# Two transformer blocks in fp32 on one core: heads retimed, SSD decay by a selector, both ends reworked, operand tiles moved to 512-byte starts

## The reference, cut to what matters

```
first block
  h = x + [SSD(32 heads, conv, gate z) | short conv] @ w_out      # hybrid mixer
      decay = exp(where(causal, a_cs[l] - a_cs[s], -inf))         # a_cs: cumulative sum of dt*a over tokens
      scores = (C @ B.T) * decay ;  y = scores @ (x * dt) + x * d_skip
  h = h + cross_attention(4 heads, 256 memory tokens)
  h = h + swiglu(h);  h = rmsnorm(h)
second block
  q,k,v of three kinds of heads:
      8 differential heads (two softmaxes each), 8 stick-breaking heads, 8 band heads with a relative bias
  each head's output normalised; x = x + y @ w_o
  x = x + swiglu with a causal conv on the gate;  out = rmsnorm(x) * final_norm_2
```

## Time and profile before

| | |
|---|---|
| median of three runs | 2810.08 us |
| profiled execution | 2806.39 us |
| its span, first to last instruction | 2804.6 us |
| mean granted TensorE clock | 0.997 |
| TensorE busy | 2757.1 us (98%) |
| VectorE busy | 1952.7 us (70%) |
| ScalarE busy | 1284.8 us (46%) |
| HBM read | 494.41 MB, 177 GB/s over the span |

### The profile page before, as it was taken

One profiled execution on the slowest core, in us unless ns is written; L12 is line 12 of the kernel. 1 busy time (PEld: TensorE's weight loads), 2 busy tenths in 40 slices (PEclk: granted clock), 3 DMA queues, 4 the chain that ended last, 5 costly groups with the idle time before them and its releaser, 6 DMA issues.

```text
span 2804.6 us, 40399 instructions
## 1 busy us (share of the span) xinstructions
PE 2757.1 (98%) x16796; PEld 2434.7 (87%) x16796; DVE 1952.7 (70%) x2416; ACT 1284.8 (46%) x1632; POOL 90.9 (3%) x67
## 2 busy tenths in 40 slices
PE   8999999999999999999999999999999999999997
PEld 7888999888888888888888888788898888888886
DVE  7777777766767665666566886576687757775775
ACT  5444545554555443444344544454454433443443
POOL 1000000000201000000000110000010000000002
PEclk9999999999999999999999999999999999999999
DMA  6555554346555555555555554344455555565553
GB/s 234 187 185 185 172 179 143 121 144 220 184 165 171 190 195 192 184 193 192 191 188 191 191 175 159 128 158 135 151 175 193 195 191 185 181 204 191 186 192 120
DMA packets 137622, 499.16 MB, mean 178 GB/s; under 512 B 15312, under 2 KB 16344, under 8 KB 137312
## 3 DMA queue, kind: packets, MB, share of 16 engines
q1 hardware_dynamic: 135792, 492.20, 52.5%
q10 hardware_dynamic: 1648, 4.39, 0.4%
HBM read 494.41 MB, written 2.11 MB: 177 GB/s over the span
## 4 chain that ended last, share of the span: by engine, by line
PE 94%; DVE 3%; ACT 2%; issue 0%; DMA 0%; DVEq 0%; ACTq 0%
PE PS L477 94%; DVE wlo L1201 1%; ACT whi L819 1%; DVE AR L1507 0%; DVE X L1635 0%; ACT AR L997 0%; DVE X L1677 0%; DMA X<-in_x 0%; PE PS L554 0%; DVE X L1633 0%; ACT AR L1065 0%; DVE H L1195 0%; DVE AR L1349 0%; DVE AR L1343 0%; DVE AR L1516 0%
## 5 line engine op out<-in xcount | busy, mean ns | idle before, releaser
L477 PE MATMUL PS<-H,whi 128*128 128x512 f32 (+1 forms) x5472 | 1787.0, 380 | 12.9 <-DVE wlo L1201 11.5
L1201 DVE TENSOR_TENSOR wlo<-raw,whi 128x1024 fp32r<-128x1024 f32 x930 | 1130.6, 1231 | 681.8 <-ACT whi L819 678.6
L819 ACT ACTIVATE whi<-raw 128x1024 fp32r<-128x1024 f32 x930 | 972.1, 1057 | 984.4 <-PE PS L477 956.3
L477 PE MATMUL PS<-H,wlo 128*128 128x256 f32 x5072 | 1413.8, 279 | 0.0
L477 PEld LDWEIGHTS PS<-H,whi 128*128 128x128 f32 x5472 | 1002.5, 188 | 220.8 <-issue 17.0
L477 PEld LDWEIGHTS PS<-H,wlo 128*128 128x128 f32 x5072 | 957.5, 189 | 2.0 <-issue 1.7
L477 PE MATMUL PS<-Y,whi 128*128 128x512 f32 (+1 forms) x2240 | 717.9, 376 | 1.1 <-DVE X L1635 0.8
L477 PE MATMUL PS<-Y,wlo 128*128 128x256 f32 x2048 | 569.0, 278 | 0.0
L477 PEld LDWEIGHTS PS<-Y,whi 128*128 128x128 f32 x2240 | 407.7, 188 | 83.9 <-DVE X L1635 2.0
L477 PEld LDWEIGHTS PS<-Y,wlo 128*128 128x128 f32 x2048 | 385.5, 188 | 0.2
L1507 DVE TENSOR_REDUCE AR<-PS 128x512 f32<-128x1024 f32 x140 | 171.5, 1225 | 14.6
(11 more groups left out here) (160 smaller groups left out, 961.9 us busy)
## 6 DMA issues: line engine op xcount, KB each, us to landing
raw<-in_ffn SPq DMA_DIRECT2D x528, 512.0 KB, 4.4
raw<-in_w_in SPq DMA_DIRECT2D x178, 512.0 KB, 4.5
raw<-in_w_qkv SPq DMA_DIRECT2D x96, 512.0 KB, 3.8
raw<-in_w_out SPq DMA_DIRECT2D x64, 512.0 KB, 4.4
raw<-in_w_o SPq DMA_DIRECT2D x40, 512.0 KB, 3.8
raw<-in_w_q SPq DMA_DIRECT2D x8, 512.0 KB, 3.9
raw<-in_w_k SPq DMA_DIRECT2D x8, 512.0 KB, 3.8
raw<-in_w_v SPq DMA_DIRECT2D x8, 512.0 KB, 4.7
```

The source lines that it names most:

```text
L477: return e.matmul(out, l, r, start=start, stop=stop)
L819: a.then_inc(e.activation(c.whi[:, s % NW, :], c.raw[:, s % NRAW, :], ACT.Copy), "whi")
L1201: v.then_inc(e.tensor_tensor(c.wlo[:, s % NW, :], c.raw[:, s % NRAW, :], c.whi[:, s % NW, :].bitcast(F32), ALU.subtract), "wlo")
```

## The change

It has five parts.

1. **Timetable.** The slots of `xa`, `dfa`, `dfb`, `stk` and `bnd` are new, with some `idle` counts one larger; waits for V, K and Q name the tile that a head needs, where before they named all tiles.
2. **SSD decay.** The `dt` task now makes the cumulative sums as rows: 32 rows of high parts, 32 of low parts, and the rest zero, in `ACS`. `SEL` is a matrix of 128 rows whose column h picks the rows of head h. A head takes one matmul of 384 columns and one of 2 x 128 for the mask. On VectorE the two instructions that add `d_skip` on the diagonals become one.
3. **Start.** The 16 gains come with `x` in one DMA, the first half of weights comes and is split in two parts, ScalarE's table is loaded before it waits, and the first four blocks wait for the first part alone.
4. **End.** ScalarE multiplies `x` by the final gain as tiles are finished; norm 6 starts three slots ahead of the end with its first two matmuls; the last table load is moved ahead; VectorE does six instructions of 512 columns and GpSimd two, and eight output DMAs of 256 KB are issued by SyncE and ScalarE.
5. **Addresses.** A tile `gap` of 384 bytes is put ahead of `raw`, and `x` with the gains (`XG`) goes behind all others. `raw`, `whi`, `wlo`, `H`, `Y` and `CR` begin at multiples of 512 bytes; they moved by 384 bytes, `H`, `Y` and `CR` by 384 bytes less 16384.

```diff
-    out += [(first_slot("wv") + 2 + 2 * h, "xa", h) for h in range(4)]
+    out += [(first_slot("wv") + s, "xa", h) for h, s in enumerate((-5, -3, 3, 5))]
...
-    out += [(v + s, "dfa", h) for h, s in enumerate((0, 5, 10, 15, 39, 44, 49, 54))]
-    out += [(after("va") + s, "dfb", h) for h, s in enumerate((1, 5, 9, 13, 24, 28, 32, 36))]
...
+    out += [(v + 7 * h, "dfa", h) for h in range(8)]
+    out += [(v + 7 * h + 13, "dfb", h) for h in range(8)]
+    out += [(v + s, "stk", i) for i, s in enumerate((57, 71, 85, 99))]
+    out += [(v + s, "bnd", i) for i, s in enumerate((105, 114, 124, 136))]
+    out += [(first_slot("g1") + 4, "norm", 5), (N_SLOT - 3, "norm", 6)]
...
+        sb("gap", [P, 96])
         self.raw = sb("raw", [P, NRAW, SUB])
...
-        self.X = sb("X", [P, 16 * T])
...
-        self.ADT = sb("ADT", [P, 4, 32], F32R)
+        self.SEL = sb("SEL", [P, 32], F32R)
         self.AR = AR = sb("AR", [P, 17352])
+        self.XG = sb("XG", [P, 16 + 16 * T])
...
     def ssd(i):
...
-            mm(bank[:, 0:384], w0[0], c.TRIr, True, False)
-            mm(bank[:, 0:384], w0[1], c.TRIr, False, False)
-            for q in range(2):
-                for o in (128, 256):
-                    mm(bank[:, o:o + 128], w1[q], c.TRIr[:, 0:128], False, False)
-            mm(bank[:, 0:128], c.Ir, c.MNr, False, False)
-            p.then_inc(mm(bank[:, 256:384], c.Ir, c.MNr, False, True), "ssd_dec")
+            mm(bank[:, 0:384], c.SEL[:, h:h + 1].to_broadcast([P, P]), c.ACS, True, False)
+            ends = bank.rearrange("p (a b) -> p a b", a=2)[:, :, 0:128]
+            p.then_inc(mm(ends, c.Ir, c.MNr.unsqueeze(1).to_broadcast([P, 2, P]), False, True), "ssd_dec")
...
     def dt(_):                                    # TensorE
+        row = bank[0:64, 128:384]
+        for o in (0, 32):
+            mm(row[o:o + 32, :], c.adt[:, 0:32], c.tri[:, 0:256], True, False)
+        for o in (0, 32):
+            last = mm(row[o:o + 32, 128:256], c.adt[:, 32:64], c.tri[:, 0:128], False, True)
...
     def bnd(i):                                   # TensorE, output of the band heads
-        for j in range(2):
-            p.wait_ge(*done("vc", j))
+        p.wait_ge(*done("vc", i // 2))
...
+        if stage == "d12":                        # ScalarE, leave
+            a.wait_ge(*a.at)
+            for k in (2 * j, 2 * j + 1):
+                a.then_inc(e.activation(c.xt(k), c.xt(k), ACT.Copy, scale=c.col("final_norm_2", k)), "scaled")
+            if j == 6:
+                load(LN_EXP)
...
-    for k in range(16):                           # VectorE, the end
-        if k % 4:
-            v.then_inc(e.scalar_tensor_tensor(c.xt(k), c.xt(k), c.col("final_norm_2", k), c.RN, ALU.mult, ALU.mult), "gain_x")
+    for i in range(6):
+        v.wait_ge("scaled", 2 * i + 2)
+        v.then_inc(times(c.xt(2 * i, 2), c.xt(2 * i, 2), c.RN), "gain_x")
```

More of the change, by code:

```diff
@@ L463, in sync_program @@
         load(w)
[L464 to L468, removed]
+    for i in range(6):
+        s.wait_ge("gain_x", i + 1)
+        e.dma_start(c.out[:, 2 * i * T:(2 * i + 2) * T], c.xt(2 * i, 2)).then_inc(c.sems["out"], 16)
+    s.wait_ge("out", 128)
     s.wait_ge("rows", 16)
@@ L484, in take, with norm_mm @@
         return c.misc[b]
[L486 to L491, removed]
+    def norm_mm(bank, s, start, stop, cols):
+        mm(bank[:, 0:T], c.ones, s[:, 0:T], start, False)
+        last = mm(bank[:, 0:T], c.ones, s[:, T:2 * T], False, stop)
         if cols:
@@ L503, in norm @@
         p.wait_ge("sum_add", 7 * n + (6 if n == 6 else 7))
+        last = norm_mm(bank, c.SUM, True, n != 6, n in (3, 4))
         if n == 6:
+            yield from idle(3)
             p.wait_ge("sq", 8 * n + 8)
-        p.then_inc(norm_mm(bank, c.SUM, c.SQ[1] if n == 6 else None, n in (3, 4)), "norm_sum")
+            last = norm_mm(bank, c.SQ[1], False, True, False)
+        p.then_inc(last, "norm_sum")
         yield
@@ L599, in xa @@
         p.then_inc(last, "xa_s")
-        yield from idle(5)
+        yield from idle(6)
         bank = take("xa", h, "t")
@@ L607, in xa @@
         p.then_inc(last, "xa_turn")
-        yield from idle(XA_PV[h] - 5)
+        yield from idle(XA_PV[h] - 6)
         bank = take("xa", h, "o")
@@ L719, in bnd @@
             p.then_inc(last, "bnd_turn")
-        yield from idle(3)
+        yield from idle(4)
         bank = take("bnd", i, "o")
-        for j in range(2):
-            p.wait_ge(*done("vc", j))
+        p.wait_ge(*done("vc", i // 2))
         for n, WT in enumerate((P0, P1)):
@@ L841, in norm @@
         _, r, col = norm_dst(c, n)
-        yield
+        yield from idle(3 if n == 6 else 1)
         if col is not None:
@@ L902, in dt @@
         a.then_inc(e.activation(ab, u1, ACT.Ln), "dt_a")
+        yield from idle(17)
+        row = c.bank("dt", 0, "n")[0:64, 128:384]
+        a.wait_ge("dt_p", 2)
+        a.then_inc(e.activation(c.ACS[0:64, 0:256], row, ACT.Copy))
+        a.then_inc(e.activation(c.ACS[0:64, 256:384], row[:, 128:256], ACT.Copy), "acs_hi")
         yield
@@ L1173, in scalar_program @@
         side.step(t)
+    for i in (6, 7):
+        a.wait_ge("pool_x", i - 5)
+        e.dma_start(c.out[:, 2 * i * T:(2 * i + 2) * T], c.xt(2 * i, 2)).then_inc(c.sems["out"], 16)
 def vector_program(e, c):
@@ L1228, in norm @@
         bank = c.bank("norm", n, "b")
+        if n == 6:
+            yield from idle(3)
         v.wait_ge("norm_sum", n + 1)
@@ L1232, in norm @@
         mean(c.SUM[:, 0:T], bank[:, 0:T], eps, "norm_mean")
-        yield from idle(2)
+        if n < 6:
+            yield from idle(2)
         if col is not None:
```

157 lines of the change are left out of this document (81 added, 76 removed).

## The result

| | before | changed |
|---|---|---|
| median of the runs | 2817.12 us (2809.82, 2824.17, 2810.08, 2824.58) | 2785.87 us (2785.51 to 2786.10, 4 runs) |
| profiled execution | 2806.39 us | 2785.78 us |
| its span | 2804.6 us | 2784.0 us |

The ratio is 0.9896 with a 95% interval of 0.9864 to 0.9928: about 1% faster. The kernel before has two times here, near 2810 and near 2824 us, and its median lies between them; beside the shorter one the changed kernel gains 24 us, where the forecast had 43. The two profiled executions are 20.6 us apart, where the working had 41. The time lies at the upper edge of the range, just inside it.

A forecast was written before the change was run, and what follows sets the result against it. TensorE, busy 98% of the span, was taken as the bound. Terms -21 (SSD), -12.5 (timetable), -2 (cross attention), -2.7 (start), -3 (end), addresses 0, sum to -41: forecast 2767 us, range 2705 to 2786.

The forecast's parts named there:

- Addresses: Tiles at multiples of 512 bytes, all block matmuls: taken as 0 us, bounds -163 and +20, farther out +65.
- Rival 1: 512-byte starts help in part, fewer crossings in operand reads: 2713, or 2720 to 2755 us, centred at 2735; chance 0.34.
- SSD: Decay in the stage of z: 1.4 us saved per pair of heads, less 1.5 once, net -21 us.
- Timetable: Second block's attention heads: 5 of 17.6 us of gaps and lost clock stay, -12.5 us; bounds 0 and -17.6.
- The 6.5 us of late exponentials: Largest cause of TensorE's waits in the second block's heads, where heads were packed five slots apart.
- The new wait at the first output of the band heads: Directly behind the block completing their V, ScalarE reaches the V tile late: 2 us of idle TensorE, released by L1095.
- Cross attention: Scores start up to 7 slots earlier: -2 of 3.15 us of gaps; bounds +1 and -3.
- Start: Ahead of the first product, table load and splits shortened: -2.7 us, first product near 8.7; bounds -1 and -3.5.
- End: Behind the last product: table load 1.28 us and VectorE's work 1.8 us saved, norm 6 nothing; -3 us.
- the quarter that GpSimd was to cost VectorE: At the end, VectorE loses a quarter of GpSimd's 3.0 us, so its last stretch takes 4.9 us.
- the forecast is wrong if that distance moves by 0.002 us or more: Sign: distance of two pairs in a steady stage stays at 0.345 us; 0.002 us alone is 13 us.
- rival 4: Side work bounds: VectorE delays TensorE in z, attention gaps only move; 2788 us, chance 0.14.

The follow-up runs named there:

- e1: Kernel before plus only the unused 384-byte tile ahead of all others: 2808.88 us, ratio 0.9997.
- e2: Changed kernel without its unused tile of 384 bytes: 2787.7 us.
- e13: Kernel before with matmuls of every two blocks ordered 512, 256, 256, 512: 2812.94 us.
- e12: Changed kernel with matmuls of every two blocks ordered 512, 256, 256, 512, first run: 2775.43 us.
- e6: Kernel before with the SSD part of the change alone: 2789.26 us.
- e7: Kernel before with the new timetable of the attention heads alone: 2811.76 us, ratio 0.9968.
- e8: Changed kernel with one extra 64-column matmul 20 slots into the second FFN: 2785.86 us.
- e14: Changed kernel with order 512, 256, 256, 512 once more, timed beside the kernel before in that order: 2776.57 us.
- e5: Changed kernel with an extra matmul of 32 to 256 columns at every 60th slot of both FFNs: 2786.38 us.

## Why the prediction was wrong

**Addresses: the value right, the chance wrong.** Taken at 0, and e1 and e2 show 0. Rival 1, at 0.34, had nothing for it but the alternation of the earlier trace rows, which is a rhythm of TensorE and no mark of addresses. The 0.027 us above the columns is not made of crossings of 512 bytes. (The prediction had 0.025: 50 / 145 counts matmuls that only reach into the window, the starts give 0.3467 us a block. The excess is 174 us in all and not 163.)

**SSD: -21, measured -20.8.** 21.7 us less in z, 0.9 more once at the new rows (0.9 us of extra time between 366 and 370 us; I had 1.5). A pair's decay, changed kernel, which answers to the earlier trace rows:

```profile
450.26 0.63 PE L560 MATMUL PS<-AR 128*128 128x128 f32 x4 [1.05 <-ACT AR L804]
450.64 0.42 PE L477 MATMUL PS<-CR,SEL 128*128 128x384 f32 x1
450.90 0.27 PE L477 MATMUL PS<-CR 128*128 128x256 f32 x1
451.01 0.34 PE L477 MATMUL PS<-CR,SEL 128*128 128x384 f32 x1
451.19 0.28 PE L477 MATMUL PS<-CR 128*128 128x256 f32 x1
451.30 0.39 PE L477 MATMUL PS<-H,whi 128*128 128x512 f32 x1
```

From 450.64 to 451.30 are 0.66 us where I had 0.57; this pair is a long one, the mean of the 16 is 0.60, and before it was 2.00. There is one wait of 1.05 us, and it isn't on VectorE but on ScalarE. With it given back, (21.7 + 1.05) / 16 = 1.42 us a pair, the 1.4 of the forecast. VectorE's diagonals, which answer to the earlier trace rows, cost 14.6 us as worked out (14.5):

```profile
L1335 DVE SCALAR_TENSOR_TENSOR AR<-AR 128x256 f32<-128x256 f32 x30 | 14.6, 485 | 1.1
```

**Timetable: -12.5, measured -10.3.** TensorE's two largest waits from 1600 to 2025 us, which answer to the earlier trace rows (total, times, longest):

```profile
PE PS L716 <- DVE AR L1512: 3.4, 2, 2.8
PE PS L477 <- ACT AR L1095: 2.7, 1, 2.7
```

Windows from the start of `va` to the second FFN (length, TensorE's busy time and matmuls, clock), of before:

```profile
1700.32:2053.13 352.81, 338.24 (x2330) 0.99 0.44 147
```

Of the changed kernel, and its one stretch at the lower clock (all columns of the earlier trace rows), which answers to the earlier trace rows:

```profile
1678.18:2020.71 342.53, 334.11 (x2329) 1.00 0.46 151
...
1950.00:1957.00 7.00, 4.55 (x19) 3.79 (x20) 4.29 (x11) 1.88 (x3) 0.00 (x0) 0.76 0.52 171
```

The 6.5 us of late exponentials are gone. The new wait at the first output of the band heads came where it was said and by the line that was said, at 2.7 us against 2. ScalarE's timeline shows the queue:

```profile
1896.80 0.48 ACT L1069 ACTIVATE AR<-PS,AR 128x256 f32<-128x256 f32 x1
...
1897.25 1.06 ACT L819 ACTIVATE whi<-raw 128x1024 fp32r<-128x1024 f32 x1
1898.20 0.85 ACT L1095 ACTIVATE AR<-PS,AR 128x256 f32<-128x256 f32 x2
```

The split is there (1.06 us), and ahead of it exponentials of the next pair, which I had left out. What I missed is 2.8 us behind the last band heads' weights (L1512) and after it the lower clock once more, 7 x 0.24 = 1.7 us. The gaps fell from 352.81 - 338.24 = 14.6 to 342.53 - 334.11 = 8.4 us, the clock's loss from 3.4 to 1.7. I had left 5 of both together, and 10.1 stayed: this is the term that was mis-sized most. Those are 6.2 + 1.7 = 7.9 of the 10.3 us; the other 2.4 are busy time of as many matmuls. The cycles don't explain them: in the order without cycles the same stages take 352.5 us in e13 and 342.1 in e12, 10.4 less. What does stays open.

**Cross attention: -2, measured -1.85.** -3.69 in `wv` and `xo`, +1.84 in `wq` and `wk`, where the scores moved: moved instructions take their time along.

**Start: -2.7, measured -3.4.** Timeline, which answers to the earlier trace rows:

```profile
8.06 0.77 PE L477 MATMUL PS<-H,whi 128*128 128x512 f32 x1 [8.06 <-DVE wlo L1681]
```

I had 8.7. In these two traces 0.9 us of it is lost again: TensorE's clock rose 5.9 us after the first product (13.9 us), before 3.7 us after it (15.2 us), so nine blocks in place of six ran at 0.64 us in place of 0.35. But that is not the edit's. With the old start, by the same reading, it rose 3.6 us after the first product in e6 and 5.9 in e7; with the new one 3.7 us after it in e8 and 3.8 in e14. The starts of e7's blocks, whose first product is at 11.53:

```profile
16.78 0.63 PE L475 MATMUL PS<-H,whi 128*128 128x512 f32 x1
...
17.42 0.40 PE L475 MATMUL PS<-H,whi 128*128 128x512 f32 x1
...
17.77 0.40 PE L475 MATMUL PS<-H,whi 128*128 128x512 f32 x1
```

Behind it, up to slot 60, the long cycle ate another 1.2 us. Both losses are luck.

**End: -3, measured -2.1.** The part behind the last slot is 3.0 us shorter. Timeline, which answers to the earlier trace rows:

```profile
2770.82 1.13 PE L477 MATMUL PS<-AR 128*128 128x256 f32 x4 [2.16 <-ACT AR L826]
...
2772.51 0.42 ACT L836 ACTIVATE AR<-AR 128x256 f32<-128x256 f32 x1 [0.80 <-DVE AR L1230]
...
2774.78 5.83 DVE L1199 TENSOR_TENSOR XG<-XG,AR 128x512 f32<-128x512 f32 x6
2774.82 3.43 POOL L1745 TENSOR_TENSOR XG<-XG,AR 128x512 f32<-128x512 f32 x2 [12.04 <-DVE AR L1239]
```

The table load is gone (1.3). VectorE's last stretch takes 5.83 in place of 6.71 us: 0.9 saved, not 1.8. By 0.69 each its six would take 4.1, so 1.7 of GpSimd's 3.43 us were lost to it, half and not a quarter. The exclusion that the Trainium skill (SBUF — State Buffer, Who interferes with whom) states would have made it 4.1 + 3.4 = 7.5, an estimate by that rule; the trace stays below it, though nearer than before. The 0.8 us that are left are four norm records that went ahead of the last products, and there they cost as much:

```profile
2764.80 1.03 PE L477 MATMUL PS<-AR 128*128 128x256 f32 x4
2765.48 0.58 PE L477 MATMUL PS<-Y,whi 128*128 128x512 f32 x1
```

The second FFN takes 746.6 us with the new end and 745.8 in e7, which has the old end and the same long cycle; in the common order of e14 and e13 it takes 736.2 and 735.3. So norm 6 saves nothing, as forecast, and 3.0 - 0.9 = 2.1 us are saved by the end as a whole. What failed here is the quarter that GpSimd was to cost VectorE.

**The step that failed.** The five terms come to 20.8 + 10.3 + 1.85 + 3.4 + 2.1 = 38.5 us in place of 41; the heads are 2.2 and the end 0.9 short. What parts 38.5 from the 20.6 of the two profiled executions is 13.9 us of the long cycle in the second FFN, 1.8 in `wo1`, 1.2 at the start and 0.9 of late clock there. The pair in the common order measured 36.4 (e14's heads gained 8.8 us, with one more stretch at the lower clock than e12). So the step that failed is none of the terms, but the sentence that a steady pair takes 0.345 us, carried over to all stages of the changed kernel. I had taken one window of one stage for a property of the machine, when the same trace held a second pace in other stages, and the times on record (2810 and 2824 us) were 14.4 us apart, an FFN's worth of it. What would show it was named ("the forecast is wrong if that distance moves by 0.002 us or more"), and it moved by 0.006. That the time still fell inside the range is luck: its upper part was made for rival 4, VectorE as the bound of z and heads whose gaps only move, and z gained 21.7 us and the heads 10.3.

**Shown and open.** Shown: the two cycles, in one program; within an FFN, jumps between them at extra matmuls and at a drain and nowhere else; that they don't depend on the start of the tiles modulo 512 bytes; another order of the matmuls in which no trace or time shows them (16 executions of four builds); the change worth 36.4 us there. Not shown: what within TensorE makes the cycles, why a resume leads to the one or the other, whether the change itself makes the long cycle in the second FFN more likely, and why the changed kernel's own four executions all lie at 2786, as if always just one FFN were in the long cycle (the traces of it and of e2, e5 and e8 all have the worth of one, though not of the same one).

## What to carry to other kernels

Where executions of one kernel fall into groups, find the stage that makes the step before weighing an edit of the same size: count the instructions of equal windows in equal stages of both traces. A stream of unequal matmuls can have several paces, and executions of one program can differ in them; time an edit with the stream in an order that has one. And compare more than two traces before a small loss is laid to an edit: the late clock at the start looked like its price and was not. Here that order, kept, is also the faster kernel: 2776.6 us beside 2785.9 (on different chips), and 1.6% under the kernel before timed with it (ratio 0.9838 [0.9824, 0.9853]).

## What the runs showed of the hardware

- TensorE's stream of 512- and 256-column fp32r matmuls repeats with a period of one or two blocks at 0.347 us, or of three at 0.353 us, at a granted clock of 1.00 in both, and keeps one of them for up to 2106 blocks. Regrouped by two blocks it takes 0.348.
- After its first product TensorE stayed at the lower clock for 3.6 to 5.9 us, whatever the start: 3.7 (before), 3.6 (e6) and 5.9 us (e7) with the first product at 11.5 us, 5.9 (changed kernel), 3.7 (e8) and 3.8 us (e14) with it at 8.1 to 8.3.
- Behind an equal wait of 1.87 us at the same place of one program the clock fell in one execution (e14, 0.76 over 7 us) and not in another (e12, 1.00).
- Two GpSimd instructions of 512 columns (3.43 us) stretched six of VectorE's from 4.1 to 5.83 us.
